# First halves evicted ahead of weight conversions, the read of query sums put ahead of rotations, and one output piece converted sooner

## What is computed

```
x = concat(meta[16], x[512])                 # block 1: 528 tokens
for l in 0, 1:                               # attention and mLSTM in parallel
    h = rms_norm(x);  z = h @ w_in[l]        # w_in: 1024 x IN_WIDTH
    aq, ak, av, ag, mq, mk, mv, mi, mf, mo, mgate = split(z)
    q, k = rope(rms_norm(aq)), rope(rms_norm(ak))      # 16 heads of 64, 2 key heads
    ya = window_sink_attention(q, k, av) * silu(ag)
    ym = rms_norm(mlstm(silu(conv(mq, mk)), mv, mi, mf)) * sigmoid(mo) * silu(mgate)
    x  = x + concat(ya, ym) @ w_out[l]
x = x[16:]                                   # block 2: 512 tokens
for l in 0, 1:
    z = rms_norm(x) @ w_in_2[l]
    ya = differential attention (8 heads) ; yb = dilated attention (3 groups,
         joined by weights softmax(lse)) ; ym = attention over 256 memory rows
    x  = x + (gates[0]*ya + gates[1]*yb + gates[2]*ym) @ w_out_2[l]
return rms_norm(x)
```

## Time and profile before

| | us |
|---|---|
| runs | 3037.66, 3030.43, 3036.69 |
| median | 3036.69 |
| profiled execution | 3035.71 |
| its span, first to last instruction | 3033.9 |
| its mean granted clock of TensorE | 0.988 |
| TensorE busy | 2940.7 |
| DVE busy | 1630.7 |
| ACT busy | 1263.1 |
| POOL busy | 186.2 |

### The profile page before, as it was taken

How to read it: one execution, slowest core, us unless ns; L and a number is a source line. 1 busy time by engine, 2 the same in 40 slices (tenths; PEclk the granted TensorE clock), 3 DMA queues, 4 the chain that set the end, 5 groups by cost and what they waited for, 6 DMA issues and landing times.

```text
span 3033.9 us, 44921 instructions
## 1 busy us (share of the span) xinstructions
PE 2940.7 (97%) x18366; PEld 2567.2 (85%) x18366; DVE 1630.7 (54%) x3259; ACT 1263.1 (42%) x2640; POOL 186.2 (6%) x207
## 2 busy tenths in 40 slices
PE   8899999999999999999999999999999999999998
PEld 7888888988889889888888888887888888878886
DVE  6777545366674553677433565235677433565234
ACT  5455423255554232466324433223466324433222
POOL 2100000020000000200000000000100000000000
PEclk9999999999999999999999999999999999999999
DMA  3111322211113222322232222323322232222232
GB/s 115 49 51 55 107 69 63 84 52 54 56 52 114 69 84 77 115 82 76 84 112 91 73 81 77 97 97 98 113 84 76 81 114 85 75 84 84 97 97 77
DMA packets 99735, 250.24 MB, mean 82 GB/s; under 512 B 8597, under 2 KB 44845, under 8 KB 99274
## 3 DMA queue, kind: packets, MB, share of 16 engines
q1 hardware_dynamic: 99530, 247.37, 25.6%
HBM read 239.60 MB, written 6.50 MB: 81 GB/s over the span
## 4 chain that ended last, share of the span: by engine, by line
PE 80%; DVE 11%; ACT 5%; issue 2%; DMA 1%; POOL 1%; DVEq 0%; POOLq 0%; SPq 0%; ACTq 0%
PE ps L92 77%; PE ps L95 3%; ACT Z L98 2%; DVE Z L101 2%; DVE Z L109 2%; DVE cl L101 1%; DVE ZR L101 1%; ACT ch L98 1%; DMA st<-in_stream_dram 1%; DVE Z L105 1%; DVE stat L122 1%; POOL stat L101 1%; DVE stat L109 1%; DVE Z L119 1%; ACT sq L98 0%
## 5 line engine op out<-in xcount | busy, mean ns | idle before, releaser
L101 DVE TENSOR_TENSOR cl<-st,ch 128x1024 fp32r<-128x1024 f32 (+1 forms) x436 | 501.2, 1158 | 644.0 <-ACT ch L98 643.5
L92 PE MATMUL ps<-hl,ch 128*128 128x264 f32 (+1 forms) x2816 | 834.2, 339 | 0.0
L92 PE MATMUL ps<-hh,ch 128*128 128x512 f32 (+1 forms) x2624 | 805.4, 347 | 25.7 <-ACT Z L98 11.0
L92 PE MATMUL ps<-hh,cl 128*128 128x512 f32 (+1 forms) x2624 | 794.2, 342 | 0.0
L98 ACT ACTIVATE ch<-st 128x1024 fp32r<-128x1024 f32 (+1 forms) x436 | 429.0, 990 | 512.4 <-PE ps L92 434.5
L92 PEld LDWEIGHTS ps<-hl,ch 128*128 128x128 f32 x2816 | 486.1, 190 | 59.3
L92 PEld LDWEIGHTS ps<-hh,ch 128*128 128x128 f32 x2624 | 454.5, 190 | 96.5 <-ACT Z L98 16.8
L92 PEld LDWEIGHTS ps<-hh,cl 128*128 128x128 f32 x2624 | 455.0, 190 | 59.0
L92 PE MATMUL ps<-ZR,ch 128*128 128x264 f32 (+2 forms) x1856 | 446.2, 337 | 5.5 <-DVE cl L101 5.1
L98 ACT ACTIVATE Z<-ps 64x128 f32<-64x128 f32 (+7 forms) x506 | 217.3, 437 | 426.8 <-PE ps L92 317.8
L92 PEld LDWEIGHTS ps<-ZR,ch 128*128 128x128 f32 x1856 | 305.2, 190 | 48.7 <-issue 12.8
(11 more groups left out here) (133 smaller groups left out, 3213.5 us busy)
## 6 DMA issues: line engine op xcount, KB each, us to landing
st<-in_stream_dram SPq DMA_DIRECT2D x372, 512.0 KB, 3.5
st<-in_stream_dram SPq DMA_DIRECT2D x64, 256.0 KB, 3.2
Z<-decay_rows SPq DMA_DIRECT2D x8, 904.0 KB, 6.5
Z<-bias_lines SPq DMA_DIRECT2D x16, 448.0 KB, 3.6
ya_spill<-Z SPq DMA_DIRECT2D x8, 512.0 KB, 4.6
Z<-ya_spill SPq DMA_DIRECT2D x2, 2048.0 KB, 7.5
Z<-in_x_dram SPq DMA_DIRECT2D x4, 512.0 KB, 5.3
Z<-in_mem_dram SPq DMA_DIRECT2D x2, 1024.0 KB, 5.9
```

What stands on the lines that cost most here:

```text
L92: return Ins(self, self.e and self.e.matmul(o, a, b, start=start, stop=stop, skip_group_check=True))
L101: return Ins(self, self.e and self.e.tensor_tensor(o, a, b, op))
```

## The change

Three things are changed, all of them in the order of steps; no step's work is changed but that `qsum` is split on POOL.

1. Behind the first half of a unit, `w` is no longer added by `proj`. The list remembers that one is owed, and `put` adds it behind the next step whose name ends in `ev`. This moves 106 of the 436 conversions behind an eviction, in the tiles of queries behind the steps of `chain` too. Second halves are as before.
2. `chain` sorts its steps by stage: `qsum` of the newest tile, then `rope`, then `ropeq` of the oldest. POOL's part of `qsum` becomes a step of its own, `qpow`, which comes behind all three.
3. In block 1, the `w` that was added behind the first `o1` of tile 0 is added ahead of the steps `ys` 6 to 13.

```diff
--- before.py
+++ after.py
@@ -294,9 +294,13 @@
     def __init__(self):
         self.o, self.plan = [], stream_plan()
         self.taken = self.converted = self.sq = self.g = self.gr = self.tg = self.sw = self.rot = 0
+        self.owed = False
 
     def put(self, *step):
         self.o.append(step)
+        if self.owed and step[0].endswith("ev"):
+            self.owed = False
+            self.weights()
 
     def take(self, *key):
         assert tuple(self.plan[self.taken][:len(key)]) == key, (self.plan[self.taken], key)
@@ -334,8 +338,11 @@
     def proj(self, key, nid, T, u, h, last=None):
         last = h == 1 if last is None else last
         self.put("proj", key, nid, T, u, h, last)
-        for _ in range(2 if last and not h else 1):
-            self.weights()
+        if last:
+            for _ in range(1 if h else 2):
+                self.weights()
+        else:
+            self.owed = True
 
     def projr(self, key, nid, u, h, k0=0, k1=8):
         self.put("projr", key, nid, u, h, k0, k1)
@@ -409,6 +416,7 @@
         def chain():
 
             todo, st["turn"] = st["turn"], []
+            todo.sort(key=lambda y: y[2])
             for t, n, x in todo:
                 if t == 8 and x == 0:
                     put("qkn", l)
@@ -417,6 +425,9 @@
                     put(("qsum", "rope", "ropeq")[x], l, t, n)
                 if x < (1 if t == 8 else 2):
                     st["turn"].append((t, n, x + 1))
+            for t, n, x in todo:
+                if t < 8 and x == 0:
+                    put("qpow", l, t)
 
         def rot(t):
             put("rot", l, t, self.rot)
@@ -569,7 +581,8 @@
             p = first[n] if n < 2 else (self.take(1, l, "out", n, 0), self.take(1, l, "out", n, 1))
             if n != 1:
                 put("o1", l, n, p, 0, 8)
-                self.weights()
+                if n:
+                    self.weights()
             if n == 0:
                 for k in (6, 7):
                     put("hn", l, k)
@@ -2609,7 +2622,7 @@
                 pool.wait_ge(("rotl", n), ("qks", l, t) if t < 8 else ("qkn", l, t))
                 pool.tensor_tensor(QF[t % 3], QF[t % 3], COS, ALU.mult).then_inc("pool_rope", ("ropec", l, t))
 
-            def qsum(l, t, n):
+            def qpow(l, t):
                 ap = RQ[:, :, 2 * t:2 * t + 2]
                 pool.wait_ge(("ms", l, t), ("ones",))
                 pool.tensor_tensor(ap, ap, P("mhalf").unsqueeze(2).to_broadcast([128, 5, 2]), ALU.pow).then_inc(
@@ -2669,7 +2682,7 @@
                 pool.wait_ge(("so",))
                 rsqrt(so[:, 8:12], 1024, ("so2",))
 
-            do = dict(sqa=sqa, dqkev=dqkev, dex=dex, hsc=hsc, memprep=memprep, dnorm=dnorm, final=final, nrml=nrml, load=load, rope=rope, qsum=qsum, vz=vz, mvones=mvones, pn=pn, bar=pool.bar)
+            do = dict(sqa=sqa, dqkev=dqkev, dex=dex, hsc=hsc, memprep=memprep, dnorm=dnorm, final=final, nrml=nrml, load=load, rope=rope, qpow=qpow, vz=vz, mvones=mvones, pn=pn, bar=pool.bar)
             for kind, *a in steps:
                 if kind in do:
                     do[kind](*a)
```

## The result

The changed kernel takes 3041.86 us in the median of 13 runs (3038.59 to 3044.76), the kernel before 3031.80 (3027.84 to 3037.66, 13 runs). The ratio is 1.0029, with a 95% interval of 1.0021 to 1.0036: slower, by 6 to 11 us. The median before had been 3036.69 of three runs; ten more brought it 5 us lower, and that alone moves the forecast's base. The change of +2.65 us that was forecast had the right sign and under a third of the size (+8.8 by the ratio).

What follows compares the result with a forecast made beforehand. The prediction took TensorE, busy 2940.7 of 3033.9 us, to bound the kernel. Its terms summed to +2.65 us, giving 3038.4 from the profiled execution or 3039.3 from the median 3036.69, so it said 3039, range 3031 to 3047.

Steps and rivals of the forecast that it cites:

- Sorted chain, stalls: Six head-pair groups, block 1: stop for the query sum goes, stop for joined queries grows to about 3.0 us; +1.6 us.
- Slow clock behind the joined stops: Head-pair groups: a slow TensorE clock stretch of 1.54 us behind five of six joined stops; +7.7 us, likeliest case, chance 0.43.
- rival 3: Head-pair groups: clock falls for two stretches instead of one behind each joined stop; +13.4 us, 3050, slower; chance 0.14.
- Starts of the layers: Block 1: earlier evictions shorten TensorE's stops (-3.35, -1.2 us) and remove two slow stretches (-3.1 us).
- The first gate unit: The stop of 2.39 us before 315.92 shrinks by only 0.2, twice: -0.4 us; the slow stretch behind it stays.
- Output piece: Before the second output tile: the 1.73 us stop mostly goes, -2.8 us, and one slow stretch at 522.20, -1.5 us.
- The log sums: Block 2, two places: a moved conversion stands behind an eviction that waits for weights; +3.4 us, and +1.5 for one slow stretch.
- The middle of the layers: Two places near the middle of each layer where POOL's work slows DVE; +0.4 us each, +0.8 us.
- The moved conversions that were priced at nothing: 102 of the 106 moved conversions, typically in block 2, still end in time where TensorE isn't waiting; 0 us.
- Rival 1: Head-pair groups: no slow clock stretches behind the joined stops; -5.0 us, 3031.6; chance 0.25.
- rival 2: Head-pair groups: joining is on time, the first stop vanishes and the second doesn't take over; -14 us, 3022.7, faster; chance 0.11.
- Rival 4: Second halves start no sooner; all terms but sorted chain and output piece near 0; 3036; chance 0.07.

Runs made afterwards that it cites:

- piece_only: The kernel before with only the output piece (w_out) converted sooner; 0.9969 of the kernel before.
- join_b1: The kernel before with output piece sooner, evictions ahead of conversions in block 1 alone, and each chain ordered read of the sum, joining, rotation; 0.9956 of the kernel before.
- join_lse: join_first with two conversions, one per layer of block 2 at the log sums, put back ahead of their evictions; 0.9960 of the kernel before.
- sort_only: The kernel before with the sorted chain alone; 1.0035 of the kernel before.
- rope_first: The changed kernel with each chain in the order rotation, read of the sum, joining; 1.0032 of the kernel before.
- join_first: The changed kernel with each chain in the order read of the sum, joining, rotation; 0.9967 of the kernel before.
- join_piece: The kernel before with output piece sooner and chains ordered read of the sum, joining, rotation, all conversions still ahead of evictions; 0.9976 of the kernel before.
- no_sort: The changed kernel with the chain back in its old order (joining, rotation, read of the sum); 0.9990 of the kernel before.
- evict_only: The kernel before with only evictions put ahead of conversions; 1.0007 of the kernel before.
- b1_no_sort: The kernel before with output piece sooner and evictions ahead of conversions in block 1 alone, chain in its old order; 0.9974 of the kernel before.

## Why the prediction was right, and where its sizes were off

The likeliest case, joined stops with slow clock behind them, is what happened; the time lies in the range, 3 us above the point. That it came so close is partly luck: the kernel before is 5 us under the base of the sum, and from its median of 3031.80 the forecast would have been 3034.5, 7 us too low. By the ratio the change is +8.8 us, 3.3 times the forecast +2.65.

- **Sorted chain, stalls.** Forecast +1.6. The stop for the sum is gone and the other grew from 1.23 to 2.99, by 1.76: for 1.21 gained that is +0.55 in the first group. The rotation's 1.41 us was right; of the 1.1 us that DVE was to gain at the read, 1.41 - 0.55 = 0.86 came. Six times 0.55 is 3.3 us, twice the forecast.
- **Slow clock behind the joined stops.** Forecast five stretches of 1.54, +7.7. All six came, and in four groups of the trace it lasted 6.8 us instead of 3.4: ten stretches of 1.54, 15.4 us. This is the mechanism of rival 3, which was priced at two stretches in all six. It is the term of the sum that was mis-sized most; with 15.4 in its place the sum would have been +10.4. Filling the stops gave 10.6 us back by the times of all runs.
- **A term that was missing.** At the start of a layer the scores now stand 2.68 us (81.53) where they didn't wait before, with slow clock behind; in the second layer 2.91 us. DVE does both tiles' rotations ahead of the first joining, and the second waits for POOL. DVE after:

```profile
77.86 0.70 DVE L101 TENSOR_TENSOR rot<-rot,cst 128x528 f32<-128x528 f32 x1
79.83 0.71 DVE L101 TENSOR_TENSOR Z<-Z,rot 128x528 f32<-128x528 f32 x1 [1.26 <-POOL Z L101]
80.45 0.17 DVE L119 COPY Z<-Z 128x16 f32<-128x16 f32 x1
80.72 0.71 DVE L101 TENSOR_TENSOR ZR<-Z,ZR 128x528 fp32r<-128x528 f32 x1
```

  It costs less than its length: the stops of 1.39 us and 2.35 us that TensorE had behind it in the kernel before, and their two slow stretches, are shorter or gone, and at 101.47 the second half starts 1.4 us sooner than before.
- **Starts of the layers.** Forecast -3.35 -3.1 -1.2 = -7.65 for both. In the first layer TensorE was 139.60 - 135.96 = 3.64 us ahead at the first group, of which 1.21 is the stop there: -2.4. In the second it came 1.7 us late (652.27 for 650.60) and was 726.63 - 723.54 = 3.1 us ahead at the first group: -3.6. A slow stretch of 13.7 us at 651.90 in the trace of before, which no part of the change speaks to, has a share in that which is not known. The slow stretch at 122.80 went, another came at 112.11 behind the stops of 1.50 and 0.75.
- **The first gate unit.** Forecast -0.4 with the slow stretch kept; the stop is 1.14 shorter, and the 48 matmuls behind it take 6.11 us, not 7.65. Too little was expected of the moved conversion: -1.14 - 1.54, less 0.7 for a wait ahead. That the slow stretch went may not be the change's doing, since piece_only had none behind an unchanged stop of 2.38 us. The chain of the changed kernel:

```profile
112.11 7.65 PE ps L92 x48
...
321.79 6.11 PE ps L92 x48
```

- **Output piece.** The stop of 1.73 is gone, as forecast, and so is the slow stretch of 522.20. The stalls were right; the time of piece_only is better than they say, by the clock.
- **The log sums.** Forecast +1.7 each and one slow stretch for the two; the wait is 2.02 for 0.26, +1.76. The step (the conversion "stands behind the waiting eviction") was right to 0.1 us. The slow stretch doesn't show in this pair of traces: the clock was low near the log sums of the two layers for 6.8 and 3.4 us before, and for 3.4 and 6.8 after. The timeline of ACT after: the eviction that waits, and both conversions behind it.

```profile
1744.88 0.60 ACT L98 ACTIVATE Z<-ps 128x512 f32<-128x512 f32 x1 [7.55 <-DVE Z L101]
1745.38 1.99 ACT L98 ACTIVATE ch<-st 128x1024 fp32r<-128x1024 f32 x2
```

- **The middle of the layers.** Forecast +0.8. Between the first gate unit and the output projection the two traces drift apart by 0.2 us in the first layer and not at all in the second.
- **The moved conversions that were priced at nothing.** Nothing speaks against it: conversions hold TensorE for 18.3 us as before, though 3.5 of them are new at the log sums, and join_b1 and join_lse agree within their intervals.

Rival 1 (no slow clock) and rival 2 (the second stop doesn't take over) fall with the windows above. Rival 4 (nothing arrives) falls too: the second halves do start sooner.

## What to carry to other kernels

Two short stops of an engine can be cheaper than one as long as their sum, where its clock falls behind a long one; an edit that only moves a stop behind another has to be priced with the clock. Where a queue holds both the last step of one chain and a middle step of the next, try what frees another engine's buffer first, the last step second and the middle step last, which was best here; a sort by stage does the first and undoes the second. And look in the list for evictions that wait for something other than their matmuls before you put anything behind them.

## What the runs showed of the hardware that was not expected

- The level of the clock behind a stop is not a function of its length alone. In the six groups of head pairs of each trace:

| stop in the group, us | kernels | groups with a slow stretch |
|---|---|---|
| 2.94 to 3.00 | changed, sort_only | 6 and 5 of 6 |
| 2.54 to 2.60 | rope_first (four of its groups) | 4 of 4 |
| 1.58 to 1.66 | join_first, join_lse, join_piece, join_b1 | 2, 2, 4 and 4 of 6 |
| 1.21 to 1.95, mostly with one of 1.2 behind | no_sort, evict_only, b1_no_sort | 1, 3 and 0 of 6 |
| 1.19 to 1.26, twice | before, piece_only | none |

  The one long stop without a slow stretch, TensorE's timeline of sort_only (the clock was 1.00 from 796 to 812 us):

```profile
802.35 0.28 PE L92 MATMUL ps<-mskb,idb 128*128 128x144 bf16 x2 [2.96 <-issue]
```

- Slow stretches come and go from one kernel's trace to the next, also where the change doesn't reach, and make several us. Before had these three (windows), of which the changed kernel has none:

```profile
651.90:665.60 13.70, 12.93 (x62) 11.08 (x61) 11.68 (x20) 4.51 (x9) 7.08 (x5) 0.50 0.22 58
1757.80:1764.60 6.80, 6.53 (x29) 5.99 (x29) 1.48 (x3) 1.79 (x3) 0.00 (x0) 0.50 0.10 38
2133.30:2136.70 3.40, 3.40 (x18) 3.40 (x17) 1.44 (x3) 1.83 (x4) 1.66 (x1) 0.50 0.55 154
```

  They also come and go from one execution to the next of one kernel: the mean clock of the kernel before was 0.987 in a run of 3038.5 us and 0.993 in one of 3028.2. The execution whose trace was kept took 3035.7 us, 4 above the median, which is why the two spans differ by 5.9 us where the medians differ by 10; and it is the likely reason that 17 us for the groups, read from one pair of traces, became 11 to 12 by the ratios. How many slow stretches one profile shows is in part a draw; several runs with their mean clock, or a stop that is filled, tell what they cost.
